# Final RMSNorm of a decoder step: three row passes moved to GpSimd, the tile order changed, and the mean and addend folded into ScalarE's root

## The reference, cut to what matters

```python
def rmsnorm(x, g):
    xf = x.astype(jnp.float32)
    y = xf * lax.rsqrt(jnp.mean(xf * xf, axis=-1, keepdims=True) + EPS)
    return (y * g.astype(jnp.float32)).astype(x.dtype)

x = x + g2[:, None] * moe(h, ...)      # the last residual
return rmsnorm(x, norm_f), ...         # the last norm
```

## Time and profile before

| what | value |
|---|---|
| time, median of 3 runs | 1014.57 us (1014.42 to 1016.05) |
| the profiled execution's own time | 1015.02 us |
| its span in the profile | 1013.2 us |
| TensorE busy in the span | 873.3 us (86%) |
| VectorE busy | 346.5 us (34%) |
| ScalarE busy | 199.3 us (20%) |
| GpSimd busy | 157.4 us (16%) |

### The profile page before, as it was taken

One profiled execution on the slowest core, in us unless ns is written; L12 is line 12 of the kernel. 1 busy time (PEld: TensorE's weight loads), 2 busy tenths in 40 slices (PEclk: granted clock), 3 DMA queues, 4 the chain that ended last, 5 costly groups with the idle time before them and its releaser, 6 DMA issues.

```text
span 1013.2 us, 13835 instructions
## 1 busy us (share of the span) xinstructions
PE 873.3 (86%) x4863; PEld 411.3 (41%) x4863; DVE 346.5 (34%) x1014; ACT 199.3 (20%) x362; POOL 157.4 (16%) x133
## 2 busy tenths in 40 slices
PE   3779999989999999899989989898969878988960
PEld 1557645554554443333333333333323333333420
DVE  1225233463456423432222332322222221332226
ACT  4100011020121122122212222221212221222123
POOL 0000073000001112212112222111212211211120
PEclk8789999989999999999999999999979998999995
DMA  8997422062369798899999999999999999998936
GB/s 323 365 320 208 166 75 85 1 259 99 123 244 365 198 369 316 316 338 366 381 375 359 385 390 382 377 364 359 396 382 376 391 394 336 381 377 317 361 62 254
DMA packets 70236, 302.33 MB, mean 298 GB/s; under 512 B 10020, under 2 KB 15348, under 8 KB 45062
## 3 DMA queue, kind: packets, MB, share of 16 engines
q1 hardware_dynamic: 48184, 206.43, 52.6%
q0 software_dynamic: 14208, 38.40, 15.0%
q10 hardware_dynamic: 7776, 56.63, 13.9%
HBM read 279.52 MB, written 35.22 MB: 311 GB/s over the span
## 4 chain that ended last, share of the span: by engine, by line
PE 43%; DMA 42%; DVE 7%; issue 4%; ACT 1%; DVEq 1%; SPq 1%; POOLq 0%; ACTq 0%
DMA moe_sums<-arena 22%; DMA arena<-in_w_exp_up 17%; PE bank L1143 12%; PE bank L1090 6%; PE bank L1165 6%; PE bank L939 5%; PE bank L917 5%; PE bank L871 2%; PE bank L855 2%; DMA arena<-in_w_ada 2%; DMA arena<-in_x_prompt 1%; PE bank L886 1%; PE bank L1110 1%; PE bank L1154 1%; DVE arena L1833 1%
## 5 line engine op out<-in xcount | busy, mean ns | idle before, releaser
L1143 PE MATMUL bank<-arena 128*32 128x512 f32 (+2 forms) x1616 | 363.1, 617 | 26.9 <-DMA arena<-in_w_exp_up 26.7
L1143 PEld LDWEIGHTS bank<-arena 128*32 128x32 f32 (+2 forms) x1616 | 120.9, 137 | 226.2 <-issue 222.6
L1165 PE MATMUL bank<-arena 128*32 128x512 f32 (+2 forms) x808 | 174.4, 596 | 4.1 <-ACT arena L1458 2.1
L795 POOL DMA_INDIRECT moe_sums<-arena x44 | 75.2, 1710 | 408.2 <-DVE arena L2032 374.2
L1165 PEld LDWEIGHTS bank<-arena 128*32 128x32 f32 (+2 forms) x808 | 57.7, 133 | 85.4 <-issue 81.2
L1471 ACT ACTIVATE arena<-arena 128x1024 f32<-128x1024 f32 x44 | 54.7, 1243 | 157.8 <-DVE arena L1833 157.6
L1832 DVE TENSOR_TENSOR arena<-bank,arena 128x512 f32<-128x512 f32 x48 | 33.3, 693 | 146.2 <-PE bank L1165 117.8
L1821 DVE TENSOR_TENSOR arena<-arena,bank 128x256 f32<-128x256 f32 x48 | 20.3, 423 | 179.1 <-ACT arena L1452 179.1
L871 PEld LDWEIGHTS bank<-arena 128*128 128x128 f32 (+1 forms) x440 | 55.6, 194 | 49.1 <-issue 24.7
L871 PE MATMUL bank<-arena 128*128 128x128 f32 (+1 forms) x440 | 62.5, 286 | 12.9 <-DVE arena L1586 10.4
L783 POOL DMA_INDIRECT arena<-h_rows,arena x46 | 47.6, 1036 | 93.7 <-DVE arena L2012 89.9
(11 more groups left out here) (254 smaller groups left out, 596.3 us busy)
## 6 DMA issues: line engine op xcount, KB each, us to landing
arena<-in_w_exp_gate SPq DMA_DIRECT2D x64, 1024.0 KB, 14.0
arena<-in_w_exp_up SPq DMA_DIRECT2D x64, 1024.0 KB, 34.7
arena<-in_w_exp_down ACTq DMA_DIRECT2D x54, 1024.0 KB, 11.9
arena<-in_w_ada SPq DMA_DIRECT2D x12, 2048.0 KB, 12.2
arena<-in_w_exp_down SPq DMA_DIRECT2D x10, 1024.0 KB, 17.9
arena<-in_w_in SPq DMA_DIRECT2D x2, 2048.0 KB, 20.7
arena<-in_w_in SPq DMA_DIRECT2D x1, 4096.0 KB, 24.0
moe_sums<-arena POOLq DMA_DIRECT2D x8, 512.0 KB, 5.3
```

What stands on the lines that cost most here:

```text
L795: pool.indirect_dma_start(out=sums, out_offset=bass.IndirectOffsetOnAxis(ap=sidx[:, par:par + 1], axis=0), in_=Y[:, (par + NT) % 2, :], in ...
L1143: ins = mm(out[c:c + m], xT[:, k, c:c + m], gu_w[q][:, :, k, :], start=(k == 0), stop=(k == KD - 1), tile_position=(0, c))
L1165: ins = mm(bank[2 + f][c:c + m, :], aT[:, par, k, c:c + m], dn_w[q][:, k, f * 512:(f + 1) * 512], start=(k == 0), stop=(k == 1), tile_posi ...
```

## The change

Five things. (1) The three passes of the sample tile go from VectorE to GpSimd, behind its last scatter. (2) The sample tile becomes the third of the order, and its loads are the second pair that SyncE issues. (3) VectorE adds tiles 0 and 1 before the first reciprocal, tile 2 ahead of the scaling of tile 1, and tile 3 ahead of the scaling of the sample tile. (4) ScalarE takes a root of a constant as soon as VectorE has written that constant, which VectorE does after its last expert step; the table of the root is so loaded there. (5) VectorE's `variance` pass goes: ScalarE's root takes the sum of squares itself, with 1/1024 as its scale and a column of EPS as its bias.

```diff
-        END_ORDER = (4, 0, 1, 2, 3)
+        END_ORDER, LOAD_ORDER = (0, 1, 4, 2, 3), (0, 4, 1, 2, 3)
+        END_PROMPT = (2, 3, 0, 4, 5)
+        eps_end = view(M + 6400, (2,))
...
# SyncE
-            for t in END_ORDER:
+            for t in LOAD_ORDER:
                 sp.dma_start(yin[0:ROWS[t], t, :], sums[t * P:t * P + ROWS[t], :]).then_inc(s_yin[t], 16)
...
# GpSimd, behind its last scatter
+            pool.wait_ge(s_nf, 48)
+            pool.wait_ge(s_yin[4], 16)
+            pool.wait_ge(s_y2[4], 16)
+            y = yin[0:NS, 4, :]
+            ch.link(pool.tensor_tensor(y, y, yin2[0:NS, 4, :], ALU.add))
+            ch.link(pool.tensor_tensor(y, y, g2_sample, ALU.mult))
+            pool.tensor_tensor(y, y, x_sb[0:NS, 4, :], ALU.add).then_inc(s_pad, 1)
...
# ScalarE
+            act.wait_ge(s_x3, 1)
+            A(eps_end[:, 1:2], eps_end[:, 0:1], ACT.Sqrt)
             for i, t in enumerate(END_ORDER):
                 R = ROWS[t]
-                act.wait_ge(s_x3, i + 1)
+                if t == 4:
+                    act.wait_ge(s_pad, 4)
+                else:
+                    act.wait_ge(s_x3, END_PROMPT[i])
                 A(squares_end[0:R, :], yin[0:R, t, :], ACT.Square, accum_out=ss[0:R, t:t + 1]).then_inc(s_ssq2, 1)
-                act.wait_ge(s_var2, NT + i + 1)
-                A(rstd[0:R, t:t + 1], rstd[0:R, t:t + 1], ACT.Sqrt).then_inc(s_std2, 1)
+                act.wait_ge(s_ssq2, NT + i + 1)
+                A(rstd[0:R, t:t + 1], ss[0:R, t:t + 1], ACT.Sqrt, scale=1.0 / D, bias=eps_end[0:R, 0:1]).then_inc(s_std2, 1)
...
# VectorE, x3_rows
-                if t < 4:
-                    TT(y, y, yin2[0:R, t, :], ALU.add).then_inc(s_x3, 1)
-                    return
-                ch.link(TT(y, y, yin2[0:R, t, :], ALU.add))
-                ch.link(TT(y, y, g2_sample, ALU.mult))
-                TT(y, y, x_sb[0:R, t, :], ALU.add).then_inc(s_x3, 1)
-
+                TT(y, y, yin2[0:R, t, :], ALU.add).then_inc(s_x3, 1)
+
+            V.memset(eps_end, EPS).then_inc(s_x3, 1)
+            x3_rows(0)
+            x3_rows(1)
             dve.wait_ge(s_nf, 48)
-            x3_rows(END_ORDER[0])
             for i, t in enumerate(END_ORDER):
                 R = ROWS[t]
-                if i + 1 < NT:
-                    x3_rows(END_ORDER[i + 1])
-                variance(slice(t, t + 1), s_ssq2, NT + i + 1, s_var2, s_std2, NT + i + 1)
-                ch.link(V.reciprocal(rstd[:, t:t + 1], rstd[:, t:t + 1]))
-                dve.wait_ge(s_x3, i + 1)
+                if i in (1, 2):
+                    x3_rows(i + 1)
+                dve.wait_ge(s_std2, NT + i + 1)
+                ch.link(V.reciprocal(rstd[0:R, t:t + 1], rstd[0:R, t:t + 1]))
+                if t < 4:
+                    dve.wait_ge(s_x3, END_PROMPT[i])
                 STT(out=yin[0:R, t, :], in0=yin[0:R, t, :], scalar=rstd[0:R, t:t + 1], in1=normf[0:R, :],
                     op0=ALU.mult, op1=ALU.mult).then_inc(s_out, 1)
```

More of the change, by code:

```diff
@@ L455, in build @@
         s_lv, s_ls, s_on, s_oT, s_cat = sem("o_var"), sem("o_std"), sem("o_normed"), sem("oT_done"), sem("cat_o")
-        s_pad, s_pool, s_pm, s_pc = sem("pool_cleared"), sem("pooled"), sem("pool_products"), sem("cat_p")
+        s_pad, s_pool, s_pm, s_pc = sem("pool_cleared_then_sample_end_rows"), sem("pooled"), sem("pool_products"), sem("cat_p")
         s_u8m, s_u8, s_ul = sem("u8_then_u_last_then_p8_done"), sem("u8_in_sbuf"), sem("u_last_in_sbuf")
```

## The result

Over 18 runs of each kernel, the changed kernel took 1016.35 us (median) and the kernel before 1012.85; the ratio is 1.0028, with a 95% interval of 1.0017 to 1.0038. That is 1.7 to 3.9 us slower. (The spread of single runs is wide, 1010.7 to 1016.3 before; the quotient of the two medians, 1.0035, lies inside the interval.) The profiled execution of the changed kernel took 1016.49 us, with a span of 1014.6.

What follows compares the result with a forecast made beforehand. It took VectorE's passes, in turn with ScalarE, to bound the end stage, not the loads. Without GpSimd -2.2 us, its passes 3.8 us later: +1.6 on the median 1014.57 gives 1016.2, range 1012.4 to 1017.5.

Steps and rivals of the forecast that it cites:

- the bound of 0.2%: Whole kernel: a measurement tells about 0.2%, 2.0 us, from no change; slower beyond that got chance 0.24.
- The 0.60 for no change: Whole kernel: chance that the result lies within 2.0 us of no change, from the forecast and Rival (c).
- Loads: End stage, second loads: tile 0's lands at 994.0, those of the later tiles at 997.4, 999.9 and 1002.4.
- The sum without GpSimd: End stage with GpSimd's passes costing VectorE nothing: last scaling ends at 1007.9, 2.2 us earlier than 1010.11.
- GpSimd's pass: Sample tile on GpSimd, 8x1024: 2.2 us a pass, from bounds of 1.9 to 2.4.
- The handover: End stage: GpSimd's and VectorE's passes exclude each other until 0.14 us before the first one's end.
- The race: End stage, about 997.4: GpSimd's second pass starts just ahead of addition 1; otherwise the order changes, the sum does not.
- ScalarE's third place: Sample tile third on ScalarE: GpSimd's end at 1002.7 plus some 1.4 us is ahead of the sample scaling at 1007.6.
- Table load and variance: End stage: the 1.28 us table load goes off the chain, beside the scatter; five variance passes of 0.14 go.
- Rival (a): End stage: no exclusion, as GpSimd works on 8 rows only; -2.2, time 1012.4, chance 0.16.
- Rival (c): End stage: VectorE's back-to-back passes keep GpSimd out until reciprocals; -0.3, time 1014.3, chance 0.10 with mixtures.
- Rival (b): GpSimd's second and third pass: full exclusion without early handover, or passes over 2.4 us; +2.6, time 1017.2, chance 0.24.

Runs made afterwards that it cites:

- e1: The changed kernel without GpSimd's three sample-tile passes, ScalarE waiting for the sample loads instead: end stage 23.78 us, ratio 0.9970.
- e5: The changed kernel, GpSimd's passes kept, with the sample tile's loads issued first instead of second: end stage 25.68 us, ratio 1.0004.
- e6: The changed kernel with GpSimd's three passes replaced by a tiny addition and three one-operand multiplications by 1.0: end stage 25.98 us, ratio 1.0007.
- e7: The changed kernel without ScalarE's early root of a constant, so without the early table load: end stage 28.32 us, ratio 1.0029.
- e4: The kernel before with parts 4 and 5 alone, sample tile still first and on VectorE: end stage 23.20 us, ratio 0.9977.
- e9: The kernel before with parts 4 and 5 alone, measured a second time: end stage 23.29 us, ratio 0.9977.
- e3: The changed kernel with the sample tile's passes back on VectorE ahead of tile 0's addition, its loads first: end stage 24.30 us, ratio 0.9971.

## Why the prediction was right or wrong

The direction and the mechanism were right: the passes moved to GpSimd come back as time in which VectorE is kept out, and they outweigh what the other parts gain. The time, 1016.35, lies in the range (1012.4 to 1017.5) and close to the 1016.2 that was forecast, but part of that closeness is luck, since the median of before moved from 1014.57 to 1012.85 over more runs. The honest comparison is by differences: +1.6 us forecast, +1.88 us in the end stage of the profiles, +1.7 to +3.9 in the ratio. The ratio's middle, 0.28%, is on the slower side of the bound of 0.2%, to which I gave 0.24, but the interval has the bound inside it, so the runs don't decide between that and no change. The 0.60 for no change was too much for a forecast that lay only 0.4 us from the bound.

Step by step. *Loads*: tile 0's second load landed at 988.81 + 5.0 = 993.8, the later ones at 997.1, 999.7 and 1002.1; shifted by the 0.45 us by which this profile runs ahead, that is 0.1 to 0.25 us later than forecast. *The sum without GpSimd*, -2.2 us: e1 gave -2.14. *GpSimd's pass*: 2.33 us undisturbed (e5), forecast 2.2 from bounds of 1.9 to 2.4; this is the term that was mis-sized. Two passes stand in front of VectorE, so it makes 2 x 0.13 = 0.26 us, about what the forecast of the end stage fell short by (1.88 against 1.6): the passes cost 4.02 us where 3.8 was forecast. *The handover*: scaling 0 began in effect at 1001.58 - 1.29 = 1000.29, and GpSimd's second pass ended at 1000.50, 0.2 us later; addition 2 began in effect at 1004.86 - 1.22 = 1003.64, 0.14 us ahead of the third's end. From the pooling heads I had 0.14. The rule of the Trainium skill (page "SBUF — State Buffer", section "Who interferes with whom"), that the second fully blocks until the first is finished, is right for these two-operand passes but for 0.13 to 0.21 us at each handover. There are four on the path (addition 1 to GpSimd's second pass, that to scaling 0, scaling 0 to the third pass, that to addition 2), 0.6 us in all, so taken word for word the rule would have given about +2.5, an estimate, and the end stage shows +1.88. For the one-operand scalings of e6 it is not right: they held scaling 0 for 0.65 us of their 2.76.

*The race* between addition 1 and GpSimd's second pass went the other way: addition 1 began at 997.07 and GpSimd's pass at 997.29, so addition 1 was not held (1.23 us), against what I had listed as a sign; as worked out, the sum is the same either way. Scaling 0 and addition 2, with 3.18 and 3.36 us, took a little more than the 1.5 to 3 us that I had listed. *ScalarE's third place*: the sample tile's root was done by 1005.28, VectorE wanted it at 1007.31; nothing lost, as forecast. *Table load and variance*: hidden and gone, as forecast (e7). But I had put the load behind VectorE's added write, and it began 4 us ahead of that, 978.62 against 982.67.

Rival (a), no exclusion on 8 rows: refuted by the 3.18 and 3.36 us of VectorE's passes and by e1. Rival (c), VectorE keeping GpSimd out by running back to back: refuted at the one place that tests it, scaling 0 to addition 2, where GpSimd's third pass, waiting, came first. Rival (b), longer passes and whole-length exclusion: its first half was partly true (2.33, still under its 2.4), its second not.

What the prediction missed is an option, not a step: it priced the five parts as a whole. Parts 4 and 5 by themselves, on the old order, are worth 2.7 us in the end stage (e4, e9). The whole change gains no more than that even with GpSimd's passes left out (2.14 us, e1), so no gain of the new order shows.

Still open: why the ratio's middle (+2.8 us) is above the +1.88 us of the two profiles. Its interval includes that value. What the change puts ahead of the scatter, the table load and VectorE's write, did not delay it: from VectorE's last expert pass to the scatter's issue it is 1.02 us in both profiles. But the issue itself lies anywhere from 979.5 to 984.2 us in the twelve profiles, so what runs ahead of the end stage varies by more than the difference sought.

## What to carry to other kernels

Before moving a pass to an idle engine, look in the trace for places where that engine and the one relieved work at the same time, and compare each pass there with others of its shape: a pass that is "busy" for more than twice its usual length was here a wait that the chain of waits did not name. Ask where the relieved engine was idle too: here VectorE waited for loads just when the sample rows were ready, so that the three passes cost nothing that shows in that place (e3) and 4.0 us on the other engine. And price the parts of a change one by one: the two small ones, a table load put early and a small pass folded into the next engine's instruction, were the gain (2.7 us in the old order).

## What the runs showed of the hardware that was not expected

GpSimd's kind of pass decides how long VectorE's two-operand passes are kept out. Beside fills (write only, 2.17 us) they ran at 1.23 and 1.29 us. Beside two-operand passes they waited until 0.14 us (additions) or 0.21 us (scaling 0) before the end. Beside GpSimd's one-operand scalings of 2.76 to 3.03 us, those that began soon after GpSimd's pass were held for a part of it: 0.65 us (1.94 for 1.29) when 0.18 us behind its start, 0.57 when 0.51 behind, nothing when 2 us behind (1.22). What in GpSimd's scaling ends its hold early, these runs don't tell. Nor do they part the time from the kind: the two passes of VectorE that were held are its scalings, the others its additions.

A pass over 8 rows cost GpSimd what a pass over 128 would by its columns: 2.33 us for 1024, where the 128-row passes of the earlier trace rows give an estimate of 1.9 to 2.4. And a root with a scale and a bias from memory took 0.29 us where the plain one took 0.20.
